# HGRN score stages: the diagonal and the five smallest levels on 32-key column tiles, scores kept compact

## The reference

```python
def chunked_gated_recurrence(q, k, log_f, v):
    # S_t = diag(f_t) S_(t-1) + k_t v_t^T,  o_t = S_t^T q_t
    ...
        b = jnp.cumsum(gi, axis=2)
        diff = b[:, :, :, None, :] - b[:, :, None, :, :]
        decay = jnp.exp(jnp.where(causal_in_chunk, diff, -jnp.inf))
        scores = jnp.einsum('nhtk,nhsk,nhtsk->nhts', qi, ki, decay)
        intra = jnp.einsum('nhts,nhsv->nhtv', scores, vi)
```

## Time and profile before

| what | us |
|---|---|
| median of 3 runs (2559.37 to 2561.64) | 2559.63 |
| the profiled execution | 2561.45 |
| its span | 2559.7 |
| TensorE matmuls busy | 2533.7 (99%) |
| VectorE busy | 1684.7 (66%) |
| ScalarE busy | 1230.4 (48%) |
| all 28 `hgrn_level` of TensorE (448 matmuls) | 58.5 |

### The profile page before, as it was taken

How to read it: one execution, slowest core, us unless ns; L and a number is a source line. 1 busy time by engine, 2 the same in 40 slices (tenths; PEclk the granted TensorE clock), 3 DMA queues, 4 the chain that set the end, 5 groups by cost and what they waited for, 6 DMA issues and landing times.

```text
span 2559.7 us, 32855 instructions
## 1 busy us (share of the span) xinstructions
PE 2533.7 (99%) x13382; PEld 2170.2 (85%) x13382; DVE 1684.7 (66%) x1813; ACT 1230.4 (48%) x1446; POOL 28.6 (1%) x26
## 2 busy tenths in 40 slices
PE   8999999999999999999999999999999999999998
PEld 6878888888888888888888888888888888888886
DVE  6645766565565555655777878785776777777777
ACT  7545345443443443444545454544555444444443
POOL 0100000000000000000000000000000000000000
PEclk9999999999999999999999999999999999999999
DMA  9444445555555555555545354445465555555553
GB/s 380 157 138 156 168 152 176 186 190 194 192 189 190 189 192 194 189 189 181 173 148 182 132 179 145 169 165 174 161 211 187 189 190 195 189 186 187 191 188 130
DMA packets 127478, 465.63 MB, mean 182 GB/s; under 512 B 14272, under 2 KB 14528, under 8 KB 126432
## 3 DMA queue, kind: packets, MB, share of 16 engines
q1 hardware_dynamic: 127328, 463.54, 52.8%
HBM read 461.38 MB, written 2.10 MB: 181 GB/s over the span
## 4 chain that ended last, share of the span: by engine, by line
PE 94%; issue 3%; DVE 1%; ACT 0%; DMA 0%; DVEq 0%; SPq 0%; POOL 0%; POOLq 0%; ACTq 0%
PE job L757 29%; PE job L764 15%; PE job L746 15%; PE job L748 14%; PE job L747 14%; PE att L949 2%; PE att L892 1%; PE att L780 0%; PE att L792 0%; PE att L961 0%; PE att L860 0%; DVE w_low L1296 0%; PE att L978 0%; PE att L975 0%; PE att L933 0%
## 5 line engine op out<-in xcount | busy, mean ns | idle before, releaser
L1296 DVE TENSOR_TENSOR w_low<-raw,w_high 128x1024 fp32r<-128x1024 f32 x856 | 1042.3, 1224 | 708.2 <-ACT w_high L1017 706.4
L1017 ACT ACTIVATE w_high<-raw 128x1024 fp32r<-128x1024 f32 x856 | 903.9, 1058 | 904.5 <-PE job L748 503.2
L757 PE MATMUL job<-actA,w_high 128*128 128x512 f32 x3328 | 836.0, 393 | 0.0
L757 PEld LDWEIGHTS job<-actA,w_high 128*128 128x128 f32 x3328 | 599.8, 189 | 108.0
L764 PEld LDWEIGHTS job<-actA,w_low 128*128 128x128 f32 x3328 | 453.9, 190 | 32.6
L746 PE MATMUL job<-w_high,actB 128*128 128x512 f32 x1184 | 463.0, 391 | 9.9 <-DVE w_low L1296 9.7
L764 PE MATMUL job<-actA,w_low 128*128 128x256 f32 x3328 | 464.0, 282 | 0.0
L747 PE MATMUL job<-w_low,actB 128*128 128x512 f32 x1184 | 461.6, 390 | 0.0
L748 PE MATMUL job<-w_high,actB 128*128 128x512 f32 x1184 | 461.4, 390 | 0.0
L746 PEld LDWEIGHTS job<-w_high,actB 128*128 128x128 f32 x1184 | 222.8, 188 | 56.4 <-DVE w_low L1296 9.9
L748 PEld LDWEIGHTS job<-w_high,actB 128*128 128x128 f32 x1184 | 222.7, 188 | 46.5
(11 more groups left out here) (201 smaller groups left out, 1232.1 us busy)
## 6 DMA issues: line engine op xcount, KB each, us to landing
raw<-in_weights SPq DMA_DIRECT2D x856, 512.0 KB, 3.3
M<-in_mem_t SPq DMA_DIRECT2D x4, 512.0 KB, 7.2
slots<-in_mem SPq DMA_DIRECT2D x2, 1024.0 KB, 14.3
M<-in_x_t SPq DMA_DIRECT2D x4, 512.0 KB, 14.0
H<-in_x SPq DMA_DIRECT2D x1, 2048.0 KB, 15.0
out<-H SPq DMA_DIRECT2D x8, 256.0 KB, 3.2
slots<-in_w_small SPq DMA_DIRECT2D x1, 1024.0 KB, 14.5
slots<-in_post_mix_g SPq DMA_DIRECT2D x1, 1024.0 KB, 4.3
```

The costliest lines, as they stand in the source:

```text
L757: nc.tensor.matmul(J[job.buf][:, x, :], w_high[:, slot, cols], act_both[job.act][:, c, :, :].rearrange("p a t -> p (a t)"), start=begins a ...
L1017: nc.scalar.activation(w_high[:, s % AHEAD, :], raw[:, s % RAW_SLOTS, :], ACT.Copy)\
L1296: nc.vector.tensor_tensor(w_low[:, s % AHEAD, :], raw[:, s % RAW_SLOTS, :], w_high[:, s % AHEAD, :].bitcast(F32), ALU.subtract).then_inc(l ...
```

## The change

The diagonal and levels 0 to 4 no longer multiply 128 tokens by 128 tokens. Each block is cut into four pieces of 32 tokens; each piece's 32 keys (the stationary operand, 128 channels by 32 columns) meet its own 32 queries, and the output goes to partitions 32b to 32b + 31 of `att`. A stage is then 32 products instead of 8, and its scores take 256 columns of one bank instead of 1024 of two. They are collected compactly in `in_block` (256 columns, in the first slot of `M`): the diagonal is evicted there, and the five picks write there, with a mask of their own, `sibling_block`. A new stage `hgrn_spread`, on ScalarE behind window 36, copies the four squares of each block to their place in `hg["diag"]`. Levels 5 and 6 are as before, and their picks wait for it.

```diff
--- before.py
+++ after.py
@@ -27,6 +27,9 @@
 HEADS4 = 4
 GROUPS = D // COLS
 LEVELS = 7
+
+BLOCK = 32
+SMALL = 5
 EPS = 1e-6
 HEAD_DIM = 128
 GLA_DK = 64
@@ -144,6 +147,7 @@
     "hgrn_diagonal": dict(scored=1, diagonal=1),
     "hgrn_level": dict(scored=1, keys_stepped=1, stepped=1, picked=1),
     "hgrn_keys": dict(keys_set=1),
+    "hgrn_spread": dict(spread=1),
     "hgrn_across": dict(scored=1, across=1),
     "hgrn_attend": dict(attended=1),
     "m_part": dict(m_set=1),
@@ -312,6 +316,7 @@
         for level in range(LEVELS):
             p.put(base + 25 + 2 * level, "hgrn_keys", level)
             p.put(base + 27 + 2 * level, "hgrn_level", level)
+        p.put(base + 36, "hgrn_spread")
         j = p.job("tokens", "A", "hgrn_w_in", 3 * D + g * COLS)
         p.put_early(j.end, "copy_job", j.buf, "v", "h")
         j = p.job("tokens", "A", "hgrn_w_in", 4 * D + g * COLS)
@@ -500,6 +505,7 @@
         ident16 = sb("ident16", [P, P], BF16)
         causal16 = sb("causal16", [P, TT, T], BF16)
         sibling = sb("sibling", [P, LEVELS, P], U8)
+        sibling_block = sb("sibling_block", [P, SMALL, BLOCK], U8)
         half = sb("half", [P, 8])
         sums = sb("sums", [P, 8])
         col_sums = sb("col_sums", [P, TT, GROUPS])
@@ -552,6 +558,8 @@
         hg = {"QP": [a_slot(1), a_slot(0)], "KS": [a_slot(2), a_slot(3)], "f": [a_slot(7), a_slot(6)],
               "q": a_slot(8), "diag": a_slot(9), "sig": m_slot(0), "kk": m_slot(1), "off": m_slot(1),
               "sq": m_slot(2)}
+
+        in_block = m_slot(0)[:, 0:8 * BLOCK]
         post_g = a2(6)
         z_conv, y_gate, y_value, y_sig, y = a_slot(0), a_slot(1), a_slot(2), a_slot(3), a_slot(4)
 
@@ -926,12 +934,11 @@
                 wait(pe, n, "hgrn_ready", 0)
                 wait(pe, n, "across", 0)
                 wait(pe, n, "rows_ready", 0)
-                for h in range(HEADS4):
-                    for t in range(TT):
-                        at = (2 * h + t) * P
-                        tok = slice(h * T + t * P, h * T + (t + 1) * P)
-                        mm = nc.tensor.matmul(att[:, at // COLS, at % COLS:at % COLS + P], hg["kk"][:, tok],
-                                              hg["q"][:, tok], start=True, stop=True)
+                for x in range(2 * HEADS4):
+                    for b in range(P // BLOCK):
+                        tok = slice(x * P + b * BLOCK, x * P + (b + 1) * BLOCK)
+                        mm = nc.tensor.matmul(att[b * BLOCK:(b + 1) * BLOCK, 0, x * BLOCK:(x + 1) * BLOCK],
+                                              hg["kk"][:, tok], hg["q"][:, tok], start=True, stop=True)
                 mm.then_inc(S["scored"], 1)
 
             def hgrn_level(level):
@@ -943,6 +950,15 @@
                 wait(pe, n, "keys_set", 0)
                 wait(pe, n, "picked", -1)
                 wait(pe, n, "o_low", 0)
+                if level < SMALL:
+                    for x in range(2 * HEADS4):
+                        for b in range(P // BLOCK):
+                            at = x * P + b * BLOCK
+                            mm = nc.tensor.matmul(att[b * BLOCK:(b + 1) * BLOCK, bank, x * BLOCK:(x + 1) * BLOCK],
+                                                  hg["sq"][:, at:at + BLOCK], crossed(0, at, BLOCK, m),
+                                                  start=True, stop=True)
+                    mm.then_inc(S["scored"], 1)
+                    return
                 for h in range(HEADS4):
                     for t in range(TT):
                         at = (2 * h + t) * P
@@ -964,6 +980,7 @@
 
             def hgrn_attend():
                 wait(pe, n, "across", 0)
+                wait(pe, n, "spread", 0)
                 wait(pe, n, "copied", 0)
                 wait(pe, n, "picked", 0)
                 wait(pe, n, "o_low", 0)
@@ -1163,8 +1180,16 @@
                     ins.then_inc(S["o_high"], 1)
                 elif name == "hgrn_diagonal":
                     wait(act, n, "scored")
+                    nc.scalar.activation(in_block, att[:, 0, 0:8 * BLOCK], ACT.Copy).then_inc(S["diagonal"], 1)
+                elif name == "hgrn_spread":
+                    wait(act, n, "picked", 0)
                     wait(act, n, "attended", 0)
-                    nc.scalar.activation(by_token(hg["diag"]), att[:, 0:2, :], ACT.Copy).then_inc(S["diagonal"], 1)
+                    for b in range(P // BLOCK):
+                        rows_ = slice(b * BLOCK, (b + 1) * BLOCK)
+                        ins = nc.scalar.activation(
+                            hg["diag"][rows_, :].rearrange("p (x c) -> p x c", c=P)[:, :, rows_],
+                            in_block[rows_, :].rearrange("p (x c) -> p x c", c=BLOCK), ACT.Copy)
+                    ins.then_inc(S["spread"], 1)
                 elif name == "hgrn_keys":
 
                     wait(act, n, "keys_stepped", 0)
@@ -1274,6 +1299,10 @@
                 nc.scalar.activation(ident16[:, :], ident[:, :], ACT.Copy).then_inc(consts16, 1)
                 nc.scalar.activation(causal16[:, :, :], causal_raw, ACT.Copy).then_inc(consts16, 1)
                 nc.scalar.activation(sibling[:, :, :], sibling_raw, ACT.Copy).then_inc(sibling_ready, 1)
+                for b in range(P // BLOCK):
+                    rows_ = slice(b * BLOCK, (b + 1) * BLOCK)
+                    ins = nc.scalar.activation(sibling_block[rows_, :, :], sibling_raw[rows_, 0:SMALL, rows_], ACT.Copy)
+                ins.then_inc(sibling_ready, 1)
                 act.wait_ge(lb_step, 1)
                 nc.scalar.activation(lb[:, :], lb[:, :], ACT.Exp).then_inc(lb_exp, 1)
 
@@ -1524,9 +1553,17 @@
                         .then_inc(S["keys_stepped"], 1)
                     nc.vector.tensor_tensor(queries, queries, block_totals(6, 2 * m - 1, 1024 - m, 1024, m), ALU.mult)\
                         .then_inc(S["stepped"], 1)
-                    pick = sibling[:, level, :].unsqueeze(1).to_broadcast([P, 8, P])
-                    nc.vector.copy_predicated(heads8(hg["diag"]), pick, att[:, bank:bank + 2, :].rearrange(
-                        "p a (x c) -> p (a x) c", c=P)).then_inc(S["picked"], 1)
+                    if level < SMALL:
+                        pick = sibling_block[:, level, :].unsqueeze(1).to_broadcast([P, 8, BLOCK])
+                        by_block = lambda ap: ap.rearrange("p (x c) -> p x c", c=BLOCK)
+                        nc.vector.copy_predicated(by_block(in_block), pick, by_block(att[:, bank, 0:8 * BLOCK]))\
+                            .then_inc(S["picked"], 1)
+                    else:
+                        wait(dve, n, "spread", 0)
+                        wait(dve, n, "attended", 0)
+                        pick = sibling[:, level, :].unsqueeze(1).to_broadcast([P, 8, P])
+                        nc.vector.copy_predicated(heads8(hg["diag"]), pick, att[:, bank:bank + 2, :].rearrange(
+                            "p a (x c) -> p (a x) c", c=P)).then_inc(S["picked"], 1)
                     if level < LEVELS - 1:
                         dve.wait_ge(S["stepped"], n.at("stepped", 1))
                         t = slots[:, 6:8, :].rearrange("p d (n two m) -> p d n two m", two=2, m=m)
@@ -1713,7 +1750,7 @@
                 nc.vector.tensor_scalar(gq_scaled[:, 1:2], V("mq_g"), HEAD_DIM ** -0.5, None, ALU.mult)\
                     .then_inc(lb_step, 1)
                 dve.wait_ge(lb_step, 7)
-                dve.wait_ge(sibling_ready, 1)
+                dve.wait_ge(sibling_ready, 2)
 
             dve.wait_ge(gains_loaded, 16)
             walk(n, lambda w: None, split, stage)
```

## The result

The changed kernel takes 2537.86 us (median of 4, 2536.16 to 2539.18) against 2559.97 before: ratio 0.9911, interval [0.9899, 0.9924].

The account below looks back on a forecast made before the run. TensorE's stream was taken to bound the kernel. Diagonal +1.82, level 0 -0.22, level 1 +1.33, levels 2 to 4 +1.68 made +4.61 us a group, +18.4 in four: 2559.6 + 18.4 = 2578.0 us, range 2548 to 2610.

Parts of the forecast that it names:

- second price: Sequencer's pace on TensorE in each changed stage: 0.03 us an instruction, 0.06 a pair, so 3.84 us for 64 pairs.
- third price: Instruction time lying ahead of a stage, subtracted from its sequencer time: 0.58 us diagonal, about 2.1 level 0, 0.92 level 1.
- The term of 3.84 us for a stage: Sequencer time for a changed stage's 64 load-matmul pairs: 128 instructions at 0.03 us, twice the whole stage of before.
- The first price: TensorE going over to narrow tiles and back: 0.34 us for each changed stage, bounds 0 and 0.7.
- What bounds the kernel: TensorE's own stream, busy 99% of the span and 94% of the chain; only time entering or leaving it moves the end.
- work saved on VectorE is worth nothing: In the score stages, 12 to 16 us saved on VectorE's 20 smaller picks would all lie beside TensorE.
- The first rival: Column tiles overlap and nothing limits their issue: faster, 2542 us at two tiles at a time, 2532 at four; chance 0.21.
- pieces under 1.2 us: Sign in the chain's 32 x 32 groups that the sequencer isn't at 0.03 us in a stream and the first rival holds.
- the diagonal as short as level 3: Sign in the changed profile that the time ahead doesn't matter and the third price is wrong.
- the across wait still at 0.8 us: Sign: TensorE's wait for level 6's pick should stay at 0.8 us in all; growth would mean VectorE is late.
- The estimate from the Trainium skill: Matmuls never start closer than about 25 ns: 64 pairs in 1.6 us, sum near zero; 62 ns a matmul gives 4.0.
- ScalarE's spread: New `hgrn_spread` on ScalarE, 2 us a group: nothing on the path, at most 8 us if its cover were gone.

Follow-up runs that it names:

- experiment 2: The changed kernel with every product of the six small stages issued twice (128 pairs, 256 instructions a stage): 2558.72 us.
- experiment 3: The changed kernel with every product of the six small stages issued four times (256 pairs, 512 instructions a stage): 2668.15 us.
- Experiment 4: The kernel before with only TensorE's 32-key column tiles, squares written in place; full eviction, full picks and old mask kept, no spread: 2542.40 us, ratio 0.9929.
- experiment 1: The changed kernel with the loop over the four 32-key pieces outside, so eight successive products use the same column group: 2566.18 us, ratio 1.0021.

## Why the prediction was wrong

**The step that failed is the second price**, the sequencer's pace, and with it the third, how much lies ahead. I read from the earlier trace rows that two loads started 0.06 us apart after a wait, with a matmul between, and took 0.03 us an instruction for a pace that holds in a stream. It is the delay of the first instructions behind a wait. The stream in the changed kernel has a pair every 0.009 us, also at level 1, which starts as soon as its wait is met, and keeps it for 128 pairs in experiment 2 and for all 256 in two stages of experiment 3. The term of 3.84 us for a stage was 0.57. With it falls the third price: next to nothing lay ahead of level 1, and its 64 pairs take no longer than level 2's. One row had pointed that way: at `gla_across` load and matmul start together, where a pace of 0.03 would set them apart. I used it for the rival and explained it away with instructions "that stand ready".

**The first price was right**: 0.34 us for the switches, measured 0.32.

**What bounds the kernel was right**, TensorE's stream, but the conclusion that work saved on VectorE is worth nothing held only for stages of the old length. Experiment 4 puts 4.5 to 5.3 us on it. I had the numbers: the earlier trace rows gives 0.92 and 1.41 us between VectorE's or ScalarE's last step and the stage; a stage ahead that is 0.9 us shorter, or 1.65 at level 0, uses that up. I subtracted that slack from the sequencer's time instead of asking what a shorter stage does to it. The new wait at level 1 (1.3 us in all) is of that kind too, and is in no term of mine.

**The first rival was the case**, with 0.21 of the chance. I gave it 1.23 us a stage with two groups at a time and 0.78 with four; it was 0.89, between, since not the array (0.111 / 4 / 4 = 0.007 us a pair) but something at 0.009 sets the pace. Its time, 2532 to 2542, held the result, but my range began at 2548 and so left out both of its ends. What the 0.009 is stays open. Three of the things I said would show it did: pieces under 1.2 us, the diagonal as short as level 3, the across wait still at 0.8 us.

**The estimate from the Trainium skill** of 25 ns between matmuls as a floor ("TensorE: Matmul & The Clock Gate", "Wait — 56ns, not 53.3ns?") does not hold across column groups: 9 ns. In one group it was 27 ns (experiment 1), which is the array's own time. The 62 ns of the same section, with which I had found my row to agree, did not bind here either: a load and its matmul together take 9 ns. The same page's Part 3, with some 4 ns between tiles, was nearer (a pair every 9 ns here), and is what I should have given more weight, since it is the one on tiles.

**ScalarE's spread** was hidden, as forecast: no wait of TensorE's names it, and VectorE did not idle before the picks that wait for it.

## What to carry to other kernels

Small stationary operands gained from column tiles here only with successive products in different column groups (experiment 1): put the group in the innermost loop. Price the way into and out of narrow tiles (0.32 us here), and set stages on tiles side by side. When the bounding engine's stage gets shorter, recompute the slack of every engine that feeds the next stage: here a fifth of the gain or a little more hung on VectorE, which had not been waited for before at these levels, and another 3.6 us lay in a wait on a PSUM bank that another bank removed. A delay seen just after a wait is no throughput.

## What the runs showed of the hardware that I had not expected

- Load-matmul pairs of f32, 32 x 32, on four column groups in turn start every 0.009 us, whether or not the stage has just come out of a wait, and for up to 256 pairs in a row; in one group every 0.027; 64 x 64 on two groups every 0.030.
- Queries that alternate between two tiles at every element still cost on narrow tiles: level 0 covers 0.89 us for level 2's 0.76 (0.011 a pair), and 2.66 for 1.78 at full width.
- TensorE stops inside long bursts: with 256 instructions in a stage four of 24 stages do, for 0.6 to 2.2 us, with 512 all but two, for 1.2 to 4.2 us a stage. Each stop ends 1.1 to 1.5 us after the end of a 16 KB packet of instructions, so the burst has in all likelihood used up the instructions that were at hand.
